# Eighteen places instead of eleven for the experts' weights, six of them opened before the mixers are over

## The reference

```python
def expert_choice_ffn(h, w_router, w_gate, w_up, w_down):
    b, s, _ = h.shape
    cap = max(1, EC_FACTOR * s // N_EXPERTS)
    logits = jnp.einsum('bsd,de->bse', h, w_router).astype(jnp.float32)
    aff = jax.nn.softmax(logits, axis=-1)
    g, idx = lax.top_k(jnp.swapaxes(aff, 1, 2), cap)
    bidx = jnp.arange(b)[:, None, None]
    xe = h[bidx, idx]
    a = jnp.einsum('becd,edf->becf', xe, w_gate)
    u = jnp.einsum('becd,edf->becf', xe, w_up)
    ye = jnp.einsum('becf,efd->becd', jax.nn.silu(a) * u, w_down)
    ye = ye * g[..., None].astype(ye.dtype)
    return jnp.zeros_like(h).at[bidx, idx].add(ye)

def hybrid_layer(...):
    ...
    merged = (gate[:, :, 0] * (o_da @ w_da_o)
              + gate[:, :, 1] * (o_wa @ w_wa_o)
              + gate[:, :, 2] * (o_xa @ w_xa_o))
    x = x + merged @ w_out
    h2 = rmsnorm(x, ffn_norm_g)
    return x + expert_choice_ffn(h2, w_router, w_exp_gate, w_exp_up, w_exp_down)
```

## Time and profile before

| | us |
|---|---|
| median of 3 runs | 2969.28 (2966.99 to 2969.99) |
| the profiled execution, its own time | 2965.62 |
| its span, first to last instruction | 2963.5 |
| PE busy | 2461.7 (83%) |
| PEld busy | 1726.1 (58%) |
| DVE busy | 1239.3 (42%) |
| ACT busy | 970.8 (33%) |
| POOL busy | 62.3 (2%) |
| HBM read | 694.58 MB |

### The profile page before, as it was taken

The page is one execution under the profiler, slowest core; times in us unless marked ns, Lnnn a source line. Parts: engine busy times, 40 slices in busy tenths (PEclk is TensorE's granted clock), DMA queues, the critical chain, the costliest instruction groups (busy, mean ns, idle before and its releaser), DMA issues.

```text
span 2963.5 us, 39518 instructions
## 1 busy us (share of the span) xinstructions
PE 2461.7 (83%) x17250; PEld 1726.1 (58%) x17250; DVE 1239.3 (42%) x1754; ACT 970.8 (33%) x1545; POOL 62.3 (2%) x36
## 2 busy tenths in 40 slices
PE   6998997666666667666588889999999998887998
PEld 6998895111111111111277777889788887776787
DVE  4466653000000100000255655567654656754654
ACT  4557641000000000000145464434444443643442
POOL 0000010000000000000000000000000000023000
PEclk8999998776777776767789999999999999999999
DMA  5553335999999999999634335566655654331552
GB/s 193 171 157 114 129 129 232 416 418 418 418 416 416 418 418 417 416 418 418 254 100 114 100 114 188 181 211 201 203 181 183 206 178 157 109 96 52 178 178 106
DMA packets 326316, 698.19 MB, mean 236 GB/s; under 512 B 35424, under 2 KB 244576, under 8 KB 291456
## 3 DMA queue, kind: packets, MB, share of 16 engines
q1 hardware_dynamic: 322688, 679.32, 61.8%
q0 software_dynamic: 2016, 13.67, 1.2%
q10 hardware_dynamic: 1440, 2.68, 0.2%
HBM read 694.58 MB, written 1.05 MB: 235 GB/s over the span
## 4 chain that ended last, share of the span: by engine, by line
PE 57%; DMA 29%; DVE 7%; ACT 4%; issue 1%; ACTq 0%; POOL 0%; DVEq 0%; SPq 0%
PE ps L522 16%; PE ps L524 15%; PE ps L523 15%; DMA af<-in_w_exp_down 10%; DMA af<-in_w_exp_gate 10%; DMA af<-in_w_exp_up 9%; DVE ar L508 1%; PE ps L2125 1%; PE ps L1399 1%; PE ps L748 1%; PE ps L1019 1%; PE ps L1430 1%; PE ps L869 1%; PE ps L1742 1%; ACT ar L487 1%
## 5 line engine op out<-in xcount | busy, mean ns | idle before, releaser
L522 PE MATMUL ps<-ar 128*128 128x256 f32 (+1 forms) x2944 | 992.1, 337 | 70.6 <-DVE ar L508 41.1
L523 PE MATMUL ps<-ar 128*128 128x256 f32 (+1 forms) x2944 | 973.8, 331 | 0.0
L524 PE MATMUL ps<-ar 128*128 128x256 f32 (+1 forms) x2944 | 973.6, 331 | 0.0
L508 DVE TENSOR_TENSOR ar<-af,ar 128x1024 fp32r<-128x1024 f32 x520 | 612.2, 1229 | 339.9 <-ACT ar L487 339.9
L522 PEld LDWEIGHTS ps<-ar 128*128 128x128 f32 x2944 | 570.7, 194 | 139.2 <-DVE ar L508 43.3
L523 PEld LDWEIGHTS ps<-ar 128*128 128x128 f32 x2944 | 571.8, 194 | 47.0 <-issue 0.5
L524 PEld LDWEIGHTS ps<-ar 128*128 128x128 f32 x2944 | 570.7, 194 | 48.7
L487 ACT ACTIVATE ar<-af 128x1024 fp32r<-128x1024 f32 x520 | 515.1, 1049 | 152.2 <-PE ps L524 149.8
L1399 PE MATMUL ps<-af 128*32 128x512 f32 x2048 | 374.4, 826 | 191.4 <-DMA af<-in_w_exp_gate 95.8
L1399 PEld LDWEIGHTS ps<-af 128*32 128x32 f32 x2048 | 49.7, 124 | 501.7 <-DMA af<-in_w_exp_up 246.6
L1430 PE MATMUL ps<-af 128*32 128x512 f32 x1024 | 198.0, 889 | 89.4 <-DMA af<-in_w_exp_down 75.3
(11 more groups left out here) (279 smaller groups left out, 1629.3 us busy)
## 6 DMA issues: line engine op xcount, KB each, us to landing
af<-in_w_exp_gate SPq DMA_DIRECT2D x128, 1024.0 KB, 25.3
af<-in_w_exp_up SPq DMA_DIRECT2D x128, 1024.0 KB, 24.8
af<-in_w_exp_down SPq DMA_DIRECT2D x128, 1024.0 KB, 21.5
af<-in_ffn_w_in SPq DMA_DIRECT2D x88, 1024.0 KB, 5.8
af<-in_ffn_w_out SPq DMA_DIRECT2D x44, 1024.0 KB, 5.1
af<-in_w_in SPq DMA_DIRECT2D x33, 1024.0 KB, 5.1
af<-in_sgu_w_in SPq DMA_DIRECT2D x16, 1024.0 KB, 7.8
af<-in_w_out SPq DMA_DIRECT2D x12, 1024.0 KB, 5.0
```

The lines of the kernel that those rows point to most:

```text
L508: e.tensor_tensor(self.WL[load.pair][:, c], self.base(i)[:, c], f_(self.WH[load.pair][:, c]), ALU.subtract).then_inc(*self.dve.inc(("lo", ...
L522: e.matmul(o, lh, rh, start=start, stop=False, skip_group_check=True)
L523: e.matmul(o, lh, rl, start=False, stop=False, skip_group_check=True)
L524: return e.matmul(o, ll, rh, start=False, stop=stop, skip_group_check=True)
```

## The change

- Places: eighteen for the experts (4 to 17 and the dense layers' four), in the order of `EXPERT_SLOTS`. The new ones lie in units 40 to 45 (scratch of the attentions), 20, 26, 28, 14 and 30.
- Opening: the first six (`AHEAD`) wait for the mark `xo_in` instead of the end of the mixers. Place 16 (the memory of h2) waits for the transposes of h2, place 17 for the transposes of the positions. The others still wait for `over("mix")`, places 0 to 3 for the split of the `out` tile before.
- Order: `sync` goes by `self.order`, in which the four `out` tiles alternate with the first four of the experts' tiles and two more follow.
- The router's weights get a corner of the small buffer `sm`, a load of their own ahead of the `out` tiles, and a semaphore.
- `XE` holds two groups instead of four; group g lies in half g % 2. `GT`, `YE` and the silu's buffer `S1` (now `ES`) move.

```diff
-SLOT_UNIT = {0: 32, 1: 34, 2: 36, 3: 38, 4: 0, 5: 2, 6: 4, 7: 6, 8: 8, 9: 10, 10: 28, 11: 30}
+SLOT_UNIT = {0: 32, 1: 34, 2: 36, 3: 38, 4: 0, 5: 2, 6: 4, 7: 6, 8: 8, 9: 10, 10: 40, 11: 42, 12: 44, 13: 20,
+             14: 26, 15: 28, 16: 14, 17: 30}
+EXPERT_SLOTS = (8, 9, 10, 11, 12, 13, 0, 1, 2, 3, 4, 5, 6, 7, 14, 15, 16, 17)
+AHEAD = 6
...
-        slots.extend(range(4, 11))
-        self.at["router"] = len(self.loads)
-        add([(lambda q: q[:, 0:128].rearrange("p (k n) -> p k n", k=8), rows(A["w_router"]))])
+        slots[:], count[0] = EXPERT_SLOTS, 0
         for x in range(16):
...
-        del slots[4:]
+        slots[:], count[0] = range(4), 0
...
+        out, ahead = self.at["out"], self.at["gate_up", 0]
+        mixed = [q for i in range(AHEAD) for q in ([out + i] if i < 4 else []) + [ahead + i]]
+        self.order = [*range(out), *mixed, *range(ahead + AHEAD, len(self.loads))]
+
+    def slot_opens(self, slot):
+
+        if slot in EXPERT_SLOTS[0:AHEAD]:
+            return self.over("xo_in")
+        if slot == 16:
+            return [self.pe.val(("ps", "h2", 1, 1))]
+        if slot == 17:
+            return [self.pe.val(("ps", "posT"))]
+        return self.over("mix")
...
-        opened = set()
-        for q, load in enumerate(self.loads):
+        for q in self.order:
+            load = self.loads[q]
+            if q == self.at["out"]:
+                for w in S.new(self.dve.val("lam_sums")):
+                    e.wait_ge(*w)
+                e.dma_start(self.WR, A["w_router"].rearrange("(k p) n -> p k n", p=P)).then_inc(*self.router_in.one())
...
-            elif load.slot >= 4 and load.slot not in opened:
-                opened.add(load.slot)
-                for w in S.new(*self.over("mix")):
+            elif load.slot >= 4:
+                for w in S.new(*self.slot_opens(load.slot)):
                     e.wait_ge(*w)
...
-        self.XE = B(3, 2).rearrange("p (d c) -> p d c", d=8)
-        self.GT = [B(7)[:, o:o + T] for o in (0, T)]
-        self.YE = [B(7)[:, o:o + 512] for o in (512, 1024)]
+        self.GT = [B(5)[:, o:o + T] for o in (1536, 1792)]
+        self.XE = B(3).rearrange("p (g d c) -> p g d c", g=2, d=8)
         self.AT_ = [B(6)[:, o:o + 512] for o in (0, 512)]
+        self.YE = [B(6)[:, o:o + 512] for o in (1024, 1536)]
+        self.ES = [self.tw[:, o:o + 512] for o in (1024, 1536)]
+        self.WR = self.sm[:, 32:160].rearrange("p (k n) -> p k n", k=8)
...
-                for w in self.Tw.new(*free, dve.val(("ffn", "o", k)), self.loads[q].value):
+                for w in self.Tw.new(*free, dve.val(("ffn", "o", k)), (self.router_in, 16)):
...
-            q, c = self.at["gate_up", x], 32 * x
+            q, c, XE = self.at["gate_up", x], 32 * (x % 4), self.XE[:, x // 4 % 2]
...
-                        t = e.matmul(ps[32 * j:32 * j + 32, bb, :], self.XE[:, k, c:c + 32], self.base(q)[:, 512 * j:512 * j + 512],
+                        t = e.matmul(ps[32 * j:32 * j + 32, bb, :], XE[:, k, c:c + 32], self.base(q)[:, 512 * j:512 * j + 512],
...
-            e.activation(self.XE[:, 4:8, g * P:(g + 1) * P], g4(self.bank(("xe", g, 1))), ACT.Copy).then_inc(*act.inc(("xe", g, 1)))
+            e.activation(self.XE[:, g % 2, 4:8, :], g4(self.bank(("xe", g, 1))), ACT.Copy).then_inc(*act.inc(("xe", g, 1)))
```

More of the change, by code:

```diff
@@ L240, in __init__ @@
         self.side = Landed(sem("side_landed")), Landed(sem("side2_landed"))
+        self.router_in = Landed(sem("router_landed"))
         self.late_in, self.rows_in = Landed(sem("late_landed")), Landed(sem("norm_rows_landed"))
@@ L1348, in t_moe @@
         self.t_rms(e, "ffn", self.B(9), KB)
-        q, b = self.at["router"], KB.next()
-        wr = self.base(q)[:, 0:128].rearrange("p (k n) -> p k n", k=8)
+        b = KB.next()
         free = self.take(b, "logits", (dve, "logits"))
@@ L1353, in t_moe @@
             for k in range(8):
-                for w in self.Tw.new(*free, dve.val(("ffn", "o", k)), self.loads[q].value):
+                for w in self.Tw.new(*free, dve.val(("ffn", "o", k)), (self.router_in, 16)):
                     e.wait_ge(*w)
-                t = e.matmul(ps[:, b, tt * 16:tt * 16 + 16], F(self.h2)[:, k, tt * P:(tt + 1) * P], wr[:, k, :], start=k == 0, stop=k == 7)
-        t.then_inc(*pe.inc(("ps", "logits"), ("raw", q)))
+                t = e.matmul(ps[:, b, tt * 16:tt * 16 + 16], F(self.h2)[:, k, tt * P:(tt + 1) * P], self.WR[:, k, :], start=k == 0, stop=k == 7)
+        t.then_inc(*pe.inc(("ps", "logits")))
         self.t_to_tm(e, "h2", F(self.h2), Ring(*[(b + i) % 8 for i in range(1, 5)]), [dve.val(("ffn", "o", 7))])
@@ L1413, in t_moe @@
             free = self.take(b, ("prodT", x), (dve, ("prodT", x)))
-            S1 = self.tw[:, (x % 2) * 512:(x % 2 + 1) * 512]
+            S1 = self.ES[x % 2]
             for i in range(4):
@@ L1532, in gather @@
                 e.wait_ge(*w)
-            e.tensor_copy(self.XE[:, 0:4, g * P:(g + 1) * P], g4(self.bank(("xe", g, 0)))).then_inc(*dve.inc(("xe", g, 0)))
+            e.tensor_copy(self.XE[:, g % 2, 0:4, :], g4(self.bank(("xe", g, 0)))).then_inc(*dve.inc(("xe", g, 0)))
         gather(0)
@@ L2810, in begin @@
             count.n, count.dry = 0, dry
-        for landed in (*self.landed, *self.side, self.first_in, self.rest_in, self.late_in, self.rows_in):
+        for landed in (*self.landed, *self.side, self.first_in, self.rest_in, self.late_in, self.rows_in, self.router_in):
             landed.n = 0
```

## The result

| | before | after |
|---|---|---|
| median, us | 2969.64 (4 runs, 2966.99 to 2974.99) | 2953.78 (4 runs, 2949.85 to 2954.59) |
| the profiled execution's span | 2963.5 | 2951.8 |
| first expert matmul | 502.60 | 505.04 |
| last expert tile landed | 1448.34 | 1433.20 |

The ratio is 0.9942, with a 95% interval of 0.9924 to 0.9959: 12 to 23 us less, and the medians differ by 15.9. The forecast was 2951.6.

What follows compares the result with a forecast made beforehand. The expert stage was taken to be bound by its weight stream at 2.523 us a tile; seven more tiles in stock save 17.7 us, all other terms zero, so 2969.3 - 17.7 = 2951.6 us, range 2945 to 2958.

Steps and rivals of the forecast that it cites:

- The rival of no change: Expert stage bound by something else, such as TensorE, once the stock is larger: 2969 us; chance 0.03.
- Step 2: Ahead of the expert stage: all 18 tiles land in time, tile 17 some 2.8 us before the first expert matmul.
- Its rival's case: Early opening gives nothing, stream runs without gap from 467.67: gain 8 us, 2961; chance 0.12 with the late-places case.
- the last two places alone coming late: Only the last two of eighteen places come too late: gain 12.6 us, 2956.7; within the rival of chance 0.12.
- Step 3: Expert stage: TensorE uses tiles faster than 2.523 us each, so place releases stay ahead and the stream does not stall.
- Step 4: Mixers' end: output projection tiles alternating with expert tiles still land 16 us before needed; no cost, 7.5 us at most.
- Steps 5 and 6: Router weights loaded earlier from the small buffer; gathered tokens for two groups, buffers moved: zero each, router 0.4 us either way.
- Step 7: SP's issue of down tiles, 3.75 us median, may be held more with 18 places; zero while the stream is full.
- Step 8: Behind the expert stage: the next block's first four loads follow tile 383 at once; hidden now and stay hidden.
- The signs of being wrong: First expert matmul after 504, pace above 2.53, DMA share below 1 in the stage, longer chain after the last landing.
- A deeper queue slowing the stream: Up to 18 queued transfers slow the expert stream: each 1% costs 9.2 us, 2979 at 3%; chance 0.03.
- A smoother restart: DMA engines' lag in the expert stream evens out: gain 21.7 us, 2947.6, or 2955.6 if it grows; chance 0.10.

Runs made afterwards that it cites:

- e1: The changed kernel with eighteen places but plain load order, none opened before the mixers are over; 2959.01 us, ratio 0.9968 to the kernel before.
- e7: The changed kernel with all six early expert tiles queued ahead of the output projection's four tiles; 2949.57 us, ratio 0.9930 to the kernel before.
- e12: The changed kernel with down weights read as 128 pieces of 8 KB instead of 256 of 4 KB, second run; 2937.01 us, ratio 0.9907 to before.

## Why the prediction was right, point by point

- *The sum as a whole.* Stock times pace: 7 places at 2.523 us, 17.7 forecast, 17.57 measured, and the law held for 8, 11, 14 and 18 places. The rival of no change falls. The whole kernel's time agrees less closely than 2953.8 against 2951.6 looks: the profiled span was forecast near 2946 and is 2951.8. Of the profile's 6.0 us too many, 3.7 do not show in the medians, because the profiled execution of before lay 3.7 us under the median that the forecast started from, and that of after at its own. That part is luck.
- *Step 2, all eighteen in time.* Right: tile 17 was released by the positions' transposes at 496.92 + 0.39 = 497.3, 7.7 us ahead of the first expert matmul; with the 5 us of a lone tile it landed some 2.7 us ahead of it, where 2.8 were forecast. That the early opening is needed was implied and is only partly so: ten tiles or four came ahead of the mixers' end in the kernels that had all eighteen, in the scratch memory or in the dense layers' places. Its rival's case, the stream from the mixers' end on, was made in e1: gain 8.9, forecast 8 (938 for S, measured 936.89). The case of the last two places alone coming late was not tried.
- *Step 3, no starving.* Right, with TensorE's first wait at 537.56 and the share at 1.02.
- *Step 4, the cover.* Right in the changed kernel: ScalarE waits for no tile, and from the first issue of an `out` tile to the mixers' end nothing grew (411.30 to 469.87 is 58.57 us, 58.83 before). e7 shows where the cover ends: at the first tile.
- *Steps 5 and 6, zero.* From the mixers' end to the first expert matmul 35.17 us against 35.35.
- *Step 7, SP held.* Right that it costs nothing, and now seen more closely, below.
- *Step 8, behind the stage, "hidden now and stay hidden".* This is the step that missed, by a little. The loads did stay hidden, but the stretch did not stay the same length: +2.1 us in N, in both profiles of the changed kernel. TensorE ran its first 40 us at a mean clock of 0.59 in place of 0.67, and all of N at 0.83 in place of 0.84; its busy time there rose by 1.4 us. The forecast had asked what changes in the instructions and loads there, and not in the clock. It is a term of 2 to 5 us with either sign: -4.6 in e7, -3.7 in e12, +2.1 here, against before.
- *The signs of being wrong.* Two of the four came up though the mechanism was right. The first expert matmul is later than 504 (505.04), but the 2.4 us are there before the early loads start. And from the last landing to the end it is 1518.6 us in place of 1515.2, step 8 and the draw of R. Neither sign separates the change from the scatter of a profile.
- *The rivals.* A deeper queue slowing the stream is refuted (2.523 us a tile), for a reason the forecast had only half: the queue did not become deeper. A smoother restart gave nothing: S is 17.57 less, not 21.7. The 358 GB/s for loads from HBM that the Trainium skill states (DMA: Bandwidth & Descriptors, "Where 436 GB/s comes from") would have given the estimate of 2.93 us a place and 20.5 us in all; the trace disagrees a second time, with 2.51 us a place and 417 GB/s on this one core.

## What to carry to other kernels

Where a stage is bound by a stream of loads, as this one is, its buffers are worth what has landed in them when the stage's first matmul starts, times the pace, once each, and no more: count the tiles in stock, and look whether an idle gap of the stream stands ahead of that matmul. How early they came and whose memory opened first made no difference here. Then look at the stream's rate by kind of tile: the tiles in pieces of 4 KB in place of 8 took 3% longer here, they are a third of the tiles, and changing them was worth half as much as seven more places of a megabyte.

## What the runs showed that was not expected

**SP's queue holds at most some eleven of these tiles, however many places there are.** The times from issue to landing are the profile page's DMA issues, of the changed kernel against 25.3 (gate) and 21.5 (down) before, and then of e12_rows_again:

```profile
af<-in_w_exp_gate SPq DMA_DIRECT2D x128, 1024.0 KB, 25.5
af<-in_w_exp_up SPq DMA_DIRECT2D x128, 1024.0 KB, 24.9
af<-in_w_exp_down SPq DMA_DIRECT2D x128, 1024.0 KB, 21.5
```

```profile
af<-in_w_exp_down SPq DMA_DIRECT2D x128, 1024.0 KB, 27.1
```

With eighteen places the time from issue to landing did not grow. It is 21.5 us, 8.5 tiles, for 256 pieces of 4 KB, and 27.1 us, 10.8 tiles at e12's 2.50 us, for 128 pieces of 8 KB. Beyond that SP is held inside the issue. In e1, where sixteen tiles are ready to be issued at once, SP's timeline shows the eleventh, twelfth and fifteenth:

```profile
475.66 0.49 SPq L481 DMA_DIRECT2D af<-in_w_exp_gate  x1
476.19 1.54 SPq L481 DMA_DIRECT2D af<-in_w_exp_up  x1
...
480.41 6.21 SPq L481 DMA_DIRECT2D af<-in_w_exp_gate  x1
```

So places beyond about eleven were worth something here only as a stock filled ahead of the stage, not as transfers in flight; what it is that holds SP the traces do not show.

**The length of the stretch behind the stage came back within 0.5 us for each kernel profiled twice, and was unforeseen.** The same work took 133.8 to 140.6 us, by the clock that TensorE was granted in it (0.89 to 0.83), and edits far ahead of it moved it either way. Why a kernel gets the one or the other was not found. Differences of up to 7 us between versions of this kernel are therefore no evidence about an edit, unless the edited stage itself is measured.
